# Decode steps of a hybrid decoder trunk: gate function, gate product, small loads and norms moved between blocks

## The reference, cut to what matters

```
o_g = rmsnorm(o_g, gla_norm_g) * silu(gr)              # GLA output gate, 1024 + 8 tokens
log_f = log_sigmoid(mf + ml_gate_b[1]); i_pre = mi + ml_gate_b[0]
m_t = max(log_f + m_0, i_pre)                          # one decode step, per sample and head
C_t = exp(log_f + m_0 - m_t) C_0 + exp(i_pre - m_t) k v^T;   n_t the same with k
h   = C_t^T q / max(|n_t . q|, exp(-m_t))
o_m = sigmoid(mo) * (rmsnorm(h, ml_norm_g) + ml_skip * u_act)
S_t = diag(a_t) S_0 + k^T v;   o = q S_t               # the GLA step
```

## Time and profile before

| what | value |
|---|---|
| median of 3 runs | 2057.97 us (2055.84 to 2064.03) |
| the profiled execution, its own time | 2060.44 us |
| its span | 2058.7 us |
| mean granted TensorE clock | 0.923 |
| PE, DVE, ACT, POOL busy | 88%, 54%, 31%, 6% |
| `mlstm_prompt` / `decode_steps` / `decode_tail` start | 1037.7 / 1091.5 / 1139.4 us |
| `mix_and_mixer` starts | 1186.0 us |

### The profile page before, as it was taken

One profiled execution on the slowest core, in us unless ns is written; L12 is line 12 of the kernel. 1 busy time (PEld: TensorE's weight loads), 2 busy tenths in 40 slices (PEclk: granted clock), 3 DMA queues, 4 the chain that ended last, 5 costly groups with the idle time before them and its releaser, 6 DMA issues. The chain is left out here.

```text
span 2058.7 us, 32209 instructions
## 1 busy us (share of the span) xinstructions
PE 1810.5 (88%) x12919; PEld 1679.4 (82%) x12919; DVE 1115.2 (54%) x1984; ACT 636.6 (31%) x1136; POOL 118.4 (6%) x141
## 2 busy tenths in 40 slices
PE   6989999667888886889974478999999999999997
PEld 5989989656676775777863278999999999999997
DVE  5462662266777663555555765744445544444544
ACT  6513322144554443333223334512121111121111
POOL 0000000000000004132112120000000000000000
PEclk8989999858999997999976679999999999999999
DMA  7631143410000005554464547211111111211102
GB/s 189 87 95 32 52 154 122 112 23 21 11 12 1 1 2 219 191 175 179 140 164 66 174 154 217 77 39 59 41 41 41 41 41 43 79 41 41 41 21 83
DMA packets 172273, 170.87 MB, mean 83 GB/s; under 512 B 49788, under 2 KB 156884, under 8 KB 168452
## 3 DMA queue, kind: packets, MB, share of 16 engines
q1 hardware_dynamic: 168692, 131.54, 22.2%
q0 software_dynamic: 2304, 33.56, 4.3%
q10 hardware_dynamic: 1168, 4.26, 0.9%
HBM read 136.98 MB, written 36.56 MB: 84 GB/s over the span
## 5 line engine op out<-in xcount | busy, mean ns | idle before, releaser
L58 PE MATMUL pm<-hidH,weights 128*128 128x344 f32 x768 | 247.2, 322 | 4.4 <-DVE weights L3166 4.4
L58 PE MATMUL pm<-hH,wuH 128*128 128x344 f32 x768 | 247.1, 322 | 3.1 <-DVE wuL L3161 3.1
L59 PE MATMUL pm<-hidL,weights 128*128 128x344 f32 x768 | 246.3, 321 | 0.0
L60 PE MATMUL pm<-hidH,weights 128*128 128x344 f32 x768 | 246.0, 320 | 0.0
L60 PE MATMUL pm<-hH,wuL 128*128 128x344 f32 x768 | 245.7, 320 | 0.0
L59 PE MATMUL pm<-hL,wuH 128*128 128x344 f32 x768 | 245.6, 320 | 0.0
L58 PE MATMUL pz<-hH,winH 128*128 128x344 f32 x600 | 202.2, 337 | 11.0 <-DVE zb L830 6.5
L59 PE MATMUL pz<-hL,winH 128*128 128x344 f32 x600 | 195.7, 326 | 0.0
L60 PE MATMUL pz<-hH,winL 128*128 128x344 f32 x600 | 195.5, 326 | 0.0
L3170 DVE SCALAR_TENSOR_TENSOR act<-pm,onat 128x344 f32<-128x344 f32 x96 | 49.3, 516 | 245.9 <-PE pm L60 245.7
L3181 DVE TENSOR_TENSOR onat<-pm,onat 128x344 f32<-128x344 f32 x256 | 129.0, 513 | 70.3 <-PE pm L60 70.3
(11 more groups left out here) (592 smaller groups left out, 3556.4 us busy)
## 6 DMA issues: line engine op xcount, KB each, us to landing
uact<-in_w_up_dram SPq DMA_DIRECT2D x16, 1024.0 KB, 6.8
hs<-in_w_down_dram SPq DMA_DIRECT2D x16, 1024.0 KB, 4.9
raw<-in_w_in_dram SPq DMA_DIRECT2D x24, 512.0 KB, 3.9
vS_scratch<-page_rows SPq DMA_DIRECT2D x16, 512.0 KB, 4.8
hold<-vS_scratch SPq DMA_DIRECT2D x8, 1024.0 KB, 12.9
wo<-in_w_out_dram SPq DMA_DIRECT2D x12, 512.0 KB
act<-in_w_out_dram SPq DMA_DIRECT2D x12, 512.0 KB, 3.9
onat<-qkT_scratch SPq DMA_DIRECT2D x18, 256.0 KB, 4.1
```

What stands on the lines that cost most here:

```text
L58: nc.tensor.matmul(out, wH, mH, start=(k == 0), stop=False)
L59: nc.tensor.matmul(out, wH, mL, start=False, stop=False)
L60: last = nc.tensor.matmul(out, wL, mH, start=False, stop=(k == n - 1))
```

## The change

- `load_steps` splits. The 19 small loads (qk, n, m, gi, gf, gb) become `load_small_steps`, issued by SP in `gla_and_gather` after the second sample's stores (s == 1). n goes to a tile of its own, n0, and VectorE copies it into column 64 of Cs in `decode_steps`. The tiles are allocated before that block.
- `mo` gets its own semaphore. ScalarE takes its Sigmoid in `mlstm_prompt` behind that load alone, and GpSimd multiplies uact by mo at the end of the same block (two instructions of 128x1032) instead of in `decode_steps`.
- The gate gr is `ACT.Silu` in one instruction of ScalarE; GpSimd's product and the tile sigr go.
- In `decode_steps` the square of glas moves ahead of the wait for G_OUT on ScalarE, its sum ahead of the wait for M_DEN on VectorE, its root and reciprocal ahead of the last steps of the mLSTM's norm.
- In `decode_tail` the sum of the norm stands between turned(1) and turned(2), the reciprocal right behind turned(3).
- Two 1x1 activations are added: Exp at the end of ScalarE's stream in `mlstm_prompt`, Sigmoid at the end of that in `decode_steps`.

```diff
# gla_and_gather, SP
                         sp.dma_start(io["vS"][s, :, half * 8:half * 8 + 8, :]...).then_inc(v_stored[half], 16)
+                    if s == 1:
+                        load_small_steps(sp, io, at, small_in)
+                sp.wait_ge(small_in, 16 * SMALL_STEP_LOADS)
...
+def load_small_steps(sp, io, at, loads):
+    zT = io["zT"]
+    sp.dma_start(at["qk"][:, :, :], zT[GQ:GQ + 4 * P, T:TT].rearrange("(j p) s -> p j s", p=P)).then_inc(loads, 16)
+    for h in range(4):
+        rws, hp = slice((h % 2) * 64, (h % 2) * 64 + 64), h // 2
+        sp.dma_start(at["n0"][rws, hp, :], io["state_mlstm_n"][0, :, h, :].rearrange("s d -> d s")).then_inc(loads, 16)
+        sp.dma_start(at["m0"][rws, hp, :], ...)
+        sp.dma_start(at["gi"][rws, hp, :], zT[MI + h:MI + h + 1, T:TT].broadcast_to([64, NS])).then_inc(loads, 16)
+        sp.dma_start(at["gf"][rws, hp, :], ...)
+    for h2 in range(2):
+        sp.dma_start(at["gb"][h2 * 64:h2 * 64 + 64, :, :], ...)
+SMALL_STEP_LOADS = 1 + 4 * 4 + 2
-STEP_LOADS = 4 + 4 * 8 + 2
+STEP_LOADS = 2 + 4 * 4
# mlstm_prompt, GpSimd
                 constants_of_steps(nc, pool, keep, at, laid)
+                pool.wait_ge(mo_ready, 1)
+                uact = keep["uact"]
+                for hp in range(HP):
+                    nc.gpsimd.tensor_tensor(uact[:, hp, :], uact[:, hp, :], at["mo"][:, hp * TT:(hp + 1) * TT], ALU.mult)
# mlstm_prompt, ScalarE
-                act.wait_ge(step_in, 16 * STEP_LOADS)
-                nc.scalar.activation(at["mo"], at["mo"], ACT.Sigmoid)
+                act.wait_ge(mo_in, 16)
+                nc.scalar.activation(at["mo"], at["mo"], ACT.Sigmoid).then_inc(mo_ready, 1)
+                nc.scalar.activation(warm[:, :], keep["eps"][0:1, :], ACT.Exp)
# decode_steps, GpSimd
                 nc.gpsimd.tensor_tensor(hs..., hd..., ALU.mult)
-                nc.gpsimd.tensor_tensor(uact..., uact..., at["mo"], ALU.mult)
-                pool.wait_ge(sig_ready, 1)
-                nc.gpsimd.tensor_tensor(gated, at["gr"], at["sigr"], ALU.mult).then_inc(gated_done, 1)
                 pool.wait_ge(rnh_ready, 1)
# decode_steps, ScalarE
-                nc.scalar.activation(at["sigr"], at["gr"], ACT.Sigmoid).then_inc(sig_ready, 1)
+                nc.scalar.activation(gated, at["gr"], ACT.Silu).then_inc(gated_done, 1)
                 for r in (2, 3):
...
+                nc.scalar.activation(sqh..., glas, ACT.Square).then_inc(sqh_ready, 1)
                 act.wait_ge(G_OUT, 1)
...
                 nc.scalar.activation(pT..., PT..., ACT.Copy).then_inc(pt_copied, 1)
-                nc.scalar.activation(sqh..., glas, ACT.Square).then_inc(sqh_ready, 1)
                 act.wait_ge(G_SUM, 1)
                 nc.scalar.activation(sqo..., heads(RG, 1), ACT.Sqrt, ...).then_inc(G_RT, 1)
+                act.wait_ge(ssh_ready, 1)
+                nc.scalar.activation(ssh[:, :], ssh[:, :], ACT.Sqrt, ...).then_inc(rth_ready, 1)
                 act.wait_ge(G_NORM, 1)
...
-                act.wait_ge(ssh_ready, 1)
-                nc.scalar.activation(ssh[:, :], ssh[:, :], ACT.Sqrt, ...).then_inc(rth_ready, 1)
+                nc.scalar.activation(warm[:, :], eps[0:1, :], ACT.Sigmoid)
# decode_steps, VectorE
+                nc.vector.tensor_copy(Cs[:, :, :, 64:65], at["n0"][:, :, :].unsqueeze(3))
                 dve.wait_ge(zeroed, 1)
...
+                dve.wait_ge(sqh_ready, 1)
+                nc.vector.reduce_sum(ssh[:, :], sqh, AX.X).then_inc(ssh_ready, 1)
                 dve.wait_ge(M_DEN, 1)
...
                 nc.vector.tensor_tensor(o..., heads(RM, 0), nd..., ALU.mult).then_inc(M_DIV, 1)
-                dve.wait_ge(sqh_ready, 1)
-                nc.vector.reduce_sum(ssh[:, :], sqh, AX.X).then_inc(ssh_ready, 1)
+                dve.wait_ge(rth_ready, 1)
+                nc.vector.reciprocal(ssh[:, :], ssh[:, :]).then_inc(rnh_ready, 1)
                 dve.wait_ge(av_done, 1)
...
-                dve.wait_ge(rth_ready, 1)
-                nc.vector.reciprocal(ssh[:, :], ssh[:, :]).then_inc(rnh_ready, 1)
                 dve.wait_ge(nat_done, 1)
# decode_tail, VectorE
                 turned(1)
+                dve.wait_ge(sqh_ready, 1)
+                nc.vector.reduce_sum(ssh[:, :], sqh[:, :, :], AX.X).then_inc(ssh_ready, 1)
                 turned(2)
                 turned(3)
-                dve.wait_ge(sqh_ready, 1)
-                nc.vector.reduce_sum(ssh[:, :], sqh[:, :, :], AX.X).then_inc(ssh_ready, 1)
+                dve.wait_ge(rth_ready, 1)
+                nc.vector.reciprocal(ssh[:, :], ssh[:, :]).then_inc(rnh_ready, 1)
                 dve.wait_ge(cav_done, 1)
...
-                dve.wait_ge(rth_ready, 1)
-                nc.vector.reciprocal(ssh[:, :], ssh[:, :]).then_inc(rnh_ready, 1)
                 dve.wait_ge(av_done, 1)
```

More of the change, by code:

```diff
@@ L1932, in load_steps @@
                  io["cache_nsa_win"].rearrange("l s (p c) k h d -> p (l s) (c k h d)", c=4)).then_inc(loads, 16)
-    sp.dma_start(at["qk"][:, :, :], zT[GQ:GQ + 4 * P, T:TT].rearrange("(j p) s -> p j s", p=P)).then_inc(loads, 16)
     for h in range(4):
@@ L1939, in load_steps @@
         sp.dma_start(at["vm"][rws, hp, :, 0:64], zS[:, MV + h * 64:MV + h * 64 + 64].unsqueeze(0).broadcast_to([64, NS, 64])).then_inc(loads, 16)
-        sp.dma_start(at["Cs"][rws, hp, :, 64:65], io["state_mlstm_n"][0, :, h, :].rearrange("s (d a) -> d s a", a=1)).then_inc(loads, 16)
-        sp.dma_start(at["m0"][rws, hp, :], io["state_mlstm_m"][0, :, h:h + 1].rearrange("s a -> a s").broadcast_to([64, NS])).then_inc(loads, 16)
-        sp.dma_start(at["gi"][rws, hp, :], zT[MI + h:MI + h + 1, T:TT].broadcast_to([64, NS])).then_inc(loads, 16)
-        sp.dma_start(at["gf"][rws, hp, :], zT[MF + h:MF + h + 1, T:TT].broadcast_to([64, NS])).then_inc(loads, 16)
-    for h2 in range(2):
-        sp.dma_start(at["gb"][h2 * 64:h2 * 64 + 64, :, :],
-                     io["ml_gate_b"][0:1, :, :].rearrange("l k (a b) -> l k a b", b=2)[:, :, :, h2].broadcast_to([64, 2, HP])).then_inc(loads, 16)
-STEP_LOADS = 4 + 4 * 8 + 2
+STEP_LOADS = 2 + 4 * 4
 def constants_of_steps(nc, pool, keep, at, laid):
@@ L2020, in _ @@
             def _(sp):
-                load_steps(sp, io, at, step_in)
+                load_steps(sp, io, at, mo_in, step_in)
                 for h in range(4):
@@ L2158, in decode_steps @@
     ident, eps, ones, mixS, mqd, dcd = (keep[k] for k in ("ident", "eps", "ones", "mixS", "mqk_dec", "decay_dec"))
-    onat, hs, RN, uact = (keep[k] for k in ("onat", "hs", "rows_cols", "uact"))
+    onat, hs, RN = (keep[k] for k in ("onat", "hs", "rows_cols"))
     gated = keep["hold"][:, GATE_AT:GATE_AT + HP * TT]
@@ L2188, in decode_steps @@
                              "wpt_copied", "av_done", "reduced", "nat_done"))
-        hd_ready, gated_done, sig_ready, sqh_ready, ssh_ready, rth_ready, rnh_ready = (
-            sem(n) for n in ("hd_ready", "gated_done", "sigr_ready", "sqh_ready", "ssh_ready", "rth_ready", "rnh_ready"))
+        hd_ready, gated_done, sqh_ready, ssh_ready, rth_ready, rnh_ready = (
+            sem(n) for n in ("hd_ready", "gated_done", "sqh_ready", "ssh_ready", "rth_ready", "rnh_ready"))
         G_STATE, G_FACT, G_OUT, G_SQ, G_SUM, G_RT, G_NORM = (sem(f"dg{n}") for n in range(7))
@@ L2307, in _ @@
                         nc.scalar.activation(kT[:, r % 2, half, :], KT[half][:, :], ACT.Copy).then_inc(copied_a, 1)
+                nc.scalar.activation(sqh.rearrange("p (i h) e -> p i h e", h=4), glas, ACT.Square).then_inc(sqh_ready, 1)
                 act.wait_ge(G_OUT, 1)
@@ L2324, in _ @@
                 nc.scalar.activation(pT[:, :, :], PT[:, 0:4 * NR].rearrange("p (c r) -> p c r", c=4), ACT.Copy).then_inc(pt_copied, 1)
-                nc.scalar.activation(sqh.rearrange("p (i h) e -> p i h e", h=4), glas, ACT.Square).then_inc(sqh_ready, 1)
                 act.wait_ge(G_SUM, 1)
                 nc.scalar.activation(sqo[:, :, :, :], heads(RG, 1), ACT.Sqrt, scale=1.0 / HD, bias=eps[0:64, :]).then_inc(G_RT, 1)
+                act.wait_ge(ssh_ready, 1)
+                nc.scalar.activation(ssh[:, :], ssh[:, :], ACT.Sqrt, scale=1.0 / HD, bias=eps[:, :]).then_inc(rth_ready, 1)
                 act.wait_ge(G_NORM, 1)
@@ L2332, in _ @@
                 nc.scalar.activation(sqo[:, :, :, :], heads(RM, 2), ACT.Sqrt, scale=1.0 / HD, bias=eps[0:64, :]).then_inc(M_RT, 1)
-                act.wait_ge(ssh_ready, 1)
-                nc.scalar.activation(ssh[:, :], ssh[:, :], ACT.Sqrt, scale=1.0 / HD, bias=eps[:, :]).then_inc(rth_ready, 1)
+                nc.scalar.activation(warm[:, :], eps[0:1, :], ACT.Sigmoid)
             @block.vector
```

28 lines of the change are left out of this document (17 added, 11 removed).

## The result

The changed kernel takes 2041.61 us (2032.81 to 2055.58, 20 runs), the kernel before 2056.61 (2048.73 to 2064.55, 20 runs): ratio 0.993, 95% interval 0.9913 to 0.9947, 15.0 us between the medians. The profiled execution has a span of 2039.6 us and a mean granted clock of 0.931. So it is 0.7% faster, with an interval that leaves out 1, and its time is 5.2 us above the forecast.

What follows compares the result with a forecast made beforehand. The prediction took three blocks of short-instruction chains, each bound by its last engine, as the limit. Its terms summed to 21.55 us, taken from a median of 2057.97 to give 2036.4 us, range 2032.5 to 2044.

Steps and rivals of the forecast that it cites:

- Part 1: End of `mlstm_prompt`: Sigmoid no longer waits for the small loads, GpSimd's product ends the block; -3.5 us.
- Part 2: First half of `decode_steps`: both long GpSimd products leave and no longer stop VectorE, so G_STATE comes sooner; -8.3 us.
- Part 3: TensorE's clock in `decode_steps`: stays high for the state products and last scores once the idle stretch goes; -2.0 us.
- Part 4: Second half of `decode_steps`: square and sum leave the path, and the earlier reciprocal releases GpSimd's last product sooner; -5.7 us.
- Rival C: `gla_and_gather`: small loads share DMA engines with sample 2's gather and slow it; 3 to 8 us, 2039 to 2044; chance 0.08.
- Part 7: Small loads in `gla_and_gather`: their issue fits into SP's 29 us of idle time and costs 0.
- Part 5: Start of `decode_tail`: the Sigmoid table is loaded at the end of the block before; -0.95 us, upper bound 1.28.
- Part 6: End of `decode_tail`: the norm's sum and reciprocal come earlier, but GpSimd's product still holds a 64x64 VectorE step; -1.1 us.
- Part 8: Value loads in `decode_tail`, behind the state stores: they use up 4.5 us of slack exactly; charged 0, upper bound 3.
- signs of being wrong: `gla_and_gather` over 267 us; TensorE idle over 3 us before L2547 with loads as releaser; table load heading either block.
- A: First half of `decode_steps`: TensorE's clock stays low, so the clock gain falls away; 2038.4 us; chance 0.12.
- B: `decode_tail`: the values come late behind the state stores, their reader slipping by 3 us; 2039.4 us; chance 0.14.

Runs made afterwards that it cites:

- split_loads: Changed kernel with the 8 single-element loads (n, m) back in `mlstm_prompt`, the 11 row loads staying in `gla_and_gather`: 2040.83 us, ratio 0.9919 to the kernel before.
- mo_product_back: Changed kernel with GpSimd's product of uact and mo back in `decode_steps`, behind the product hs: 2050.68 us in one run.
- sigmoid_and_product: Changed kernel with Silu undone: ScalarE takes Sigmoid of the gate and GpSimd multiplies by the gate behind hs: 2055.06 us in one run.
- step_norms_back: Changed kernel with the GLA norm's square, sum, root and reciprocal in `decode_steps` back in their old order: 2046.65 us in one run.
- tail_two: Changed kernel; in the tail affine_select waits for ScalarE's first sigmoid and the norm's reciprocal precedes turned(2): tail 47.0 us, no total time given.
- element_loads_last: Changed kernel with the 8 single-element loads (n, m) issued behind the last sample's stores, the 11 others unmoved: 2047.45 us in one run.
- small_loads_last: Changed kernel with all 19 small loads issued behind the last sample's stores in `gla_and_gather`: 2038.57 us, ratio 0.9911 to the kernel before.
- small_loads_back: Changed kernel with all 19 small loads back in `mlstm_prompt`, behind the large ones: 2036.34 us in one run.
- early_values: Changed kernel with the values of samples 5, 6, 7 and 0 loaded before SP's wait for the state stores: 2046.31 us, ratio 0.9952 to the kernel before.
- values_first: Changed kernel with split_loads and tail_two together, plus the 4 stores of n issued behind the tail's value loads: 2034.44 us, ratio 0.989 to the kernel before.

## Why the prediction was right, and which step was wrong

The sign held, and so did the mechanisms of parts 1 to 4, which make up 19.5 of the 21.55 us. The time fell into the range, 5.2 us above the forecast. That is Rival C's place (2039 to 2044), not mine: part 7 was wrong, and parts 5, 6 and 8 were wrong in size or in what they reach.

- **Part 1, -3.5.** Measured 53.8 and 53.0 against 50.3 and 50.1: -3.2. Right. split_loads shows the margin: with 8 element loads back in the block it is 50.7, and the next block starts 0.6 us later after GpSimd's product than here. The last element load, issued at 1070.66, has come at 1084.0 if it took the longest landing of its line, 13.3, and that block starts at 1084.94.
- **Part 2, -8.3.** Right. Each long product stops VectorE for 4.3 to 4.4 us (mo_product_back, sigmoid_and_product). Silu took 1.92, as Sigmoid. The copy of n took 0.52, not 0.2, in VectorE's idle time.
- **Part 3, -2.0.** The clock stayed up; products and scores took 2.4 us less, and ScalarE's chain hides part of it. **Part 4, -5.7.** step_norms_back gives 5.7 for the order alone. Parts 2 to 4 together: 47.9 to 32.0 is -15.9, predicted -16.0.
- **Part 5, -0.95.** The table was warm, as said, but only 0.43 arrived. What failed is that I followed the branch on ScalarE and did not ask what VectorE would then meet: GpSimd's affine_select. tail_two takes that away.
- **Part 6, -1.1.** The step took 2.00 us, 1.7 of them the hold, as said, and the last 64x64 step is free (0.28). But the term didn't reach the block's length, because of part 8.
- **Part 7, 0: the step that failed.** "What hides it is SP's own idle time" was true and beside the point. I priced the loads on the queue that issues them and not on the DMA engines that the gather needs. Measured: +7.1 us (5.4 in the two traces of this kernel itself), and nothing once the loads of single elements are gone from the block. `gla_and_gather` longer than 267 us was the first of my own signs of being wrong. I had this mechanism as Rival C, at 3 to 8 us, with a chance of 0.08; the bound of 4-byte elements in the earlier trace rows, a share of 0.03 at 0 GB/s while everybody waits for the stores, was in my own rows and should have given it several times that.
- **Part 8, charged 0, bound 3.** Measured 1.7 and 2.9 us of waiting. The bound was right. "The 4.5 us of slack are used up exactly" took the stores' end at C_STATE + 17.7; SP's first load went out at + 19.2 and + 20.4.

Together: -3.2 - 15.9 + 0.2 in the three decode blocks makes -19 where -21.55 stood, and +7.1 ahead of them makes -12 (-13.5 with this kernel's own 5.4), against -15.0 and -11.6 between medians.

**Luck.** That the time lies in the range owes something to it. The high end, 2044, was made of A and B together with 2 us of C. A did not happen (the clock stayed up), and C's 7 us took the room that was kept for it: 2036.4 with C at 7.1 and B at 3 would be 2046.5, outside. The baseline helped too: the forecast started from a median of three runs, 2057.97, and the 20 runs have 2056.61. Against that median the change gave 15.0 us, 70% of the 21.55.

**What stays open.** Why element loads hold back a gather on another queue while the engines are nearly idle isn't shown, only that they do. Why the clock rises some 23.7 us into `mlstm_prompt` in most traces, and 30 to 36 us into it in three (the block then took up to 4.7 us longer), wasn't settled. Nor was the pause in the last round of element_loads_last. And three early rounds of small_loads_last were together 2.9 us too long with no small load near. In small_loads_back SP's loads of the values went out 8.3 us after the tail's start, later than in any other run; why isn't known.

## What to carry to other kernels

Look at a DMA's element size before you call its place free: here transfers of single 4-byte elements cost what ran beside or behind them (7.1 us of a block with gathers, 5 us of a queue with large loads), while their issuer, SP, had time to spare. Put them last, behind everything that somebody waits for. And when a block is shortened, ask which background transfer had been hidden by its old length.

## What the runs showed of the hardware

- With four stores of n, 2 KB each, on the queue before them, loads of 1 MB stood for 5 us at 1 GB/s and a DMA share of 0.10 (early_values). With these stores behind the loads, the loads went out at the block's start and TensorE had no wait for them (values_first).
- Of 19 small loads, the 11 whose pieces are rows cost the gathers nothing; with the 8 of single elements among them the block took 7.1 us more, part of it at a lower clock: a wait of 1.50 us for a gather was followed by a stretch at 0.50.
- GpSimd's affine_select of 1.14 us on 16 partitions held a VectorE instruction over 128 partitions for 0.85 us. The held instruction need not share a tile with it.
